# Joint mixer: attention by pairs of heads, turned modulation columns at the end, projection copies on ScalarE

## Chip, cores and metric

One core of a Trainium2 chip runs the whole program. The metric is device time of one execution in microseconds (us), the median of several runs. TensorE (PE) multiplies matrices, VectorE (DVE) and ScalarE (ACT) work on rows and on the banks that TensorE writes, GpSimd (POOL) works on rows in SBUF only, and SyncE (SP) issues the loads.

## What is computed

A float32 network of two blocks over 256 tokens of width 1024. The change touches the first layer of the second block, where 256 latent tokens and 256 context tokens are mixed by two mixers at once, from one projection:

```
aq, ak, av, ao, ag, bq, bk, bv = split_cols(h @ w_in)      # for latent and context tokens
h_ctx, h_lat = mlstm_bidirectional(...)                    # 4 heads of 128, both directions
k, q = rms_norm and rope of bk, bq                         # 8 query heads of 64, 2 key heads
b_lat = softmax([sink, q k_ctx, q k_band (windowed)]) @ v  # latent queries: 512 keys
b_ctx = softmax([sink, q_ctx k_ctx]) @ v_ctx               # context queries: 256 keys
mod   = silu(c) @ ada_w + ada_b                            # 12 parts of 1024 columns, two streams
```

The results of both mixers, side by side, go into the product with `w_out`. The modulation of this layer's later phases and of the next layer is computed in the same stage, since its 40 MB of weights have to be loaded some time.

## The kernel before

The program is one long sequence of phases. In each phase every engine has its own list of instructions, and the lists wait for each other by one counter per engine (`done(engine, phase, step, index)` is the count at which a step is finished). Dense products keep float32 accuracy with three products of split operands (lines 370 to 372); for each half slot of weights ScalarE makes the high part (`ahead`, line 357) and GpSimd the low part (line 364). Weights come through a ring of three slots of 1 MB, loaded by SyncE in the fixed order of `issue` (line 2902); a slot is loaded again when TensorE has read it.

**First projection ("2.0 in").** Six cuts of up to 512 columns, four pieces of 128 tokens each, numbered 0 to 23; a piece n is summed in bank n mod 7 and copied out by the `reader`: ScalarE for cut 4, else VectorE for even and ScalarE for odd pieces (lines 748 and 751). TensorE may start piece n when piece n - 7 is copied. Between the pieces stand the gates of the recurrent mixer (`mgate_rows_T`, `mgate_cols_T`), whose long chain of small steps runs on VectorE and ScalarE (`mgate_V`, lines 1981 to 2023), the norms of the query and key heads (`swa_prep`) and the turns of queries and keys to columns (`e0_turn`, `e1_turn`, line 860).

**The mix ("2.0 attention").** `both_of` weaves three generators on each engine, by turns: one piece of the recurrent mixer, one of the modulation, one of attention (none in each fifth turn). After 23 turns the recurrent mixer is done, and attention and modulation go on alone.

- Attention: 32 jobs, one for a head and a tile of 128 queries: first 16 over the context (256 keys, "narrow"), then 16 over latent tokens (512 keys and a mask, "wide"). At step s TensorE computes the scores of job s (line 918), turns the probabilities of job s - 3 (line 927) and multiplies those of job s - 4 with the values (line 942); VectorE takes the minimum of job s (scores are negated: lines 960, 964, 967) and scales the probabilities of job s - 2 (lines 975, 978, 981); ScalarE takes the exponentials of job s (lines 1006, 1009) and copies the turned probabilities of job s - 3 (line 1017). The probabilities have four buffers.
- Recurrent mixer: for each head h four products of queries and keys (`qk`, line 2069), which VectorE multiplies with decay tiles (line 2150) that ScalarE makes (lines 2100, 2103) from rows masked by GpSimd (line 2170), and two sums, one for each direction (line 2060), which VectorE finishes (`finish`, lines 2117 to 2134). One head takes five turns, a block.
- Modulation: 80 units, two for each 1 MB slot. `LATE_TURNS` says how many go into a turn. A part of eight units is summed in one of two banks, then VectorE adds the bias (line 1683), and TensorE turns four of six kinds of parts to columns (line 1691).

At the end TensorE turns the recurrent mixer's output (line 860), computes the gates' rows (line 1781) and starts the output projection.

## Time and profile before

| | |
|---|---|
| median of 3 runs | 1874.07 us (1873.81 to 1883.03) |
| the profiled execution | 1877.97 us, of which its span 1876.1 us |
| TensorE busy in the span | 1767.1 us |
| first product after the projection's wait | at 786.67 us |
| first modulation unit of the mix | at 866.74 us |
| first recurrent sums | at 895.03 us |
| first product of the output projection | at 1042.97 us |

Times in the rows are counted from the start of the span. A row of the timeline gives start, duration, engine, line, operation, output and inputs, how many instructions it merges, and in brackets how long the engine stood idle before and what released it. Durations of matmuls overlap: what one costs is the distance to the next start. A float32 matmul appears as two instructions.

### The profile page before, as it was taken

What the parts mean: (1) busy time and instruction counts of PE and PEld (TensorE: products, weight loads), DVE (VectorE), ACT (ScalarE), POOL (GpSimd) and SP (SyncE); (2) the same over time, 40 slices, a digit from 0 to 9 for tenths busy, and PEclk for the clock granted to TensorE, in tenths of its full rate; (3) what the DMA queues carried; (4) which work ended last, traced back from release to release, by engine and by line L of the source; (5) the groups of instructions that cost most, each with busy time, mean ns of one, the idle gap of its engine ahead of it and who ended that gap; (6) DMA issues with size and microseconds to landing.
All of it is one profiled execution on the core that took longest, in us unless ns stands there. A gap on an engine that the chain in (4) does not pass through costs nothing.

```text
span 1876.1 us, 25748 instructions
## 1 busy us (share of the span) xinstructions
PE 1767.1 (94%) x10058; PEld 1438.4 (77%) x10058; DVE 751.9 (40%) x1655; ACT 905.7 (48%) x1654; POOL 947.6 (51%) x416
## 2 busy tenths in 40 slices
PE   8999999998899999898998999999999898899998
PEld 6668998776688888785555888888888877678886
DVE  4543231244344453743567143343200443346631
ACT  4655454445566743433335354444422454457762
POOL 4645688774278885331015234444343341238886
PEclk9999999999899999999999999999999999999999
DMA  8336765443156653227875133333232430136654
GB/s 271 102 102 215 244 186 176 168 157 113 56 163 186 182 177 105 77 90 247 286 275 180 51 85 90 90 109 94 90 101 79 108 106 24 45 92 192 188 169 146
DMA packets 264843, 263.48 MB, mean 140 GB/s; under 512 B 11332, under 2 KB 202124, under 8 KB 264596
## 3 DMA queue, kind: packets, MB, share of 16 engines
q1 hardware_dynamic: 264435, 261.25, 45.0%
q8 instruction: 80, 1.31, 0.3%
q10 hardware_dynamic: 288, 0.59, 0.1%
q14 instruction: 40, 0.32, 0.1%
HBM read 260.76 MB, written 1.06 MB: 140 GB/s over the span
## 4 chain that ended last, share of the span: by engine, by line
PE 80%; DVE 7%; ACT 5%; DMA 5%; issue 2%; SPq 1%; POOL 0%; ACTq 0%; DVEq 0%
PE bank L370 18%; PE bank L371 18%; PE bank L372 17%; PE bank L1447 8%; PE bank L1448 4%; PE bank L1663 2%; PE bank L1251 2%; DMA weights<-in_ada_w 2%; ACT work L1369 1%; PE bank L1221 1%; ACT weights_high L357 1%; PE bank L2060 1%; PE bank L918 1%; PE bank L942 1%; DVE work L1330 1%
## 5 line engine op out<-in xcount | busy, mean ns | idle before, releaser
L364 POOL TENSOR_TENSOR weights_low<-weights,weights_high 128x1024 fp32r<-128x1024 f32 (+1 forms) x388 | 918.7, 2382 | 767.4 <-ACT weights_high L357 766.9
L357 ACT ACTIVATE weights_high<-weights 128x1024 fp32r<-128x1024 f32 (+1 forms) x388 | 401.6, 1046 | 377.8 <-PE bank L372 122.1
L370 PE MATMUL bank<-weights_high,normed_features_high_low 128*128 128x512 f32 (+4 forms) x752 | 288.9, 384 | 14.6 <-POOL weights_low L364 5.6
L372 PE MATMUL bank<-weights_low,normed_features_high_low 128*128 128x512 f32 (+4 forms) x752 | 273.8, 364 | 0.0
L371 PE MATMUL bank<-weights_high,normed_features_high_low 128*128 128x512 f32 (+4 forms) x752 | 273.7, 364 | 0.0
L1447 PE MATMUL bank<-normed_features_high_low,weights_high 128*128 128x512 f32 x704 | 249.4, 399 | 0.6 <-DVE normed_features_high_low L499 0.4
L370 PE MATMUL bank<-normed_features_high_low,weights_high 128*128 128x256 f32 (+1 forms) x704 | 237.9, 338 | 0.4 <-DVE normed_features_high_low L497 0.2
L371 PE MATMUL bank<-normed_features_high_low,weights_low 128*128 128x256 f32 (+1 forms) x704 | 236.5, 336 | 0.0
L372 PE MATMUL bank<-normed_features_high_low,weights_high 128*128 128x256 f32 (+1 forms) x704 | 236.5, 336 | 0.0
L1448 PE MATMUL bank<-normed_features_high_low,weights_low 128*128 128x256 f32 x704 | 197.7, 281 | 0.0
L370 PEld LDWEIGHTS bank<-weights_high,normed_features_high_low 128*128 128x128 f32 x752 | 144.9, 193 | 46.4 <-issue 13.6
L370 PE MATMUL bank<-weights_high,hidden_high 128*128 128x512 f32 x440 | 172.9, 393 | 2.8 <-DVE hidden_low_narrow L1525 1.0
L372 PE MATMUL bank<-weights_low,hidden_high 128*128 128x512 f32 x440 | 171.3, 389 | 0.0
L372 PEld LDWEIGHTS bank<-weights_low,normed_features_high_low 128*128 128x128 f32 x752 | 144.4, 192 | 21.3
L1447 PEld LDWEIGHTS bank<-normed_features_high_low,weights_high 128*128 128x128 f32 x704 | 132.3, 188 | 34.3 <-DVE normed_features_high_low L499 0.5
L371 PEld LDWEIGHTS bank<-weights_high,normed_features_high_low 128*128 128x128 f32 x752 | 145.1, 193 | 17.0
L370 PEld LDWEIGHTS bank<-normed_features_high_low,weights_high 128*128 128x128 f32 x704 | 133.6, 190 | 17.7 <-issue 3.3
L372 PEld LDWEIGHTS bank<-normed_features_high_low,weights_high 128*128 128x128 f32 x704 | 133.6, 190 | 13.6
L371 PEld LDWEIGHTS bank<-normed_features_high_low,weights_low 128*128 128x128 f32 x704 | 133.6, 190 | 13.5
L1448 PEld LDWEIGHTS bank<-normed_features_high_low,weights_low 128*128 128x128 f32 x704 | 133.0, 189 | 0.0
L371 PE MATMUL bank<-weights_high,hidden_low_narrow 128*128 128x512 f32 x264 | 102.8, 389 | 0.0
L370 PEld LDWEIGHTS bank<-weights_high,hidden_high 128*128 128x128 f32 x440 | 82.6, 188 | 23.3 <-POOL weights_low L364 2.2
(330 smaller groups left out, 2334.1 us busy)
## 6 DMA issues: line engine op xcount, KB each, us to landing
weights<-in_ffn_w_up SPq DMA_DIRECT2D x44, 1024.0 KB, 6.1
weights<-in_ffn_up SPq DMA_DIRECT2D x44, 1024.0 KB, 6.0
weights<-in_ada_w SPq DMA_DIRECT2D x40, 1024.0 KB, 6.3
weights<-in_ffn_w_down SPq DMA_DIRECT2D x20, 1024.0 KB, 5.1
weights<-in_ffn_down SPq DMA_DIRECT2D x20, 1024.0 KB, 5.0
weights<-in_diff_w_qkv SPq DMA_DIRECT2D x12, 1024.0 KB, 5.2
weights<-in_hyb_w_in SPq DMA_DIRECT2D x11, 1024.0 KB, 5.5
weights<-in_odd_w_in SPq DMA_DIRECT2D x9, 1024.0 KB, 5.2
```

The source lines that it names most:

```text
L357: A.eng.activation(high(whigh[:, m % HIGHS, :]), raw(wslot[:, u % SLOTS, :]), ACT.Copy).then_inc(scalar_done, A.one(("A", "high", m)))
L364: G.eng.tensor_tensor(raw(wlow[:, u % SLOTS, :]), raw(wslot[:, u % SLOTS, :]), high(whigh[:, m % HIGHS, :]).bitcast(F32), ALU.subtract).th ...
L370: T.eng.matmul(out_, lh, rh, start=first, stop=False)
L371: T.eng.matmul(out_, ll, rh, start=False, stop=False)
L372: return T.eng.matmul(out_, lh, rl, start=False, stop=last)
L918: i = T.eng.matmul(bank[:, a:b], l, r, start=(m == 0), stop=(m == len(terms) - 1))
L942: i = T.eng.matmul(o, l, r, start=(first and c == 0), stop=(last and c == nc_ - 1))
L1221: i = T.eng.transpose(psum[TURNED][:, at:at + P], way["probs"](buffer(way, q, x), n)[:, c * P:(c + 1) * P], ident)
L1251: i = T.eng.matmul(psum[SCORES[x]][:, a:b], l, r, start=(m == 0), stop=(m == len(terms) - 1))
L1447: T.eng.matmul(bank[:, 0:2 * n].rearrange("p (h t) -> p h t", h=2), wh, nTb[:, :, k, lo:lo + n], start=first, stop=False)
L1448: return T.eng.matmul(bank[:, 0:n], wl, nTh[:, k, lo:lo + n], start=False, stop=last)
L1663: i = T.eng.matmul(to[32 * j:32 * j + 32, :], silu_k[:, k, 2 - 2 * layer:34 - 2 * layer], w[:, a, j * MOD_N:(j + 1) * MOD_N], start=(k == ...
```

## The change

- `tile_pairs` makes 16 steps of two heads each out of the 32 jobs. A step has two halves, and each half is one turn of the weave. First half of step s: TensorE computes both heads' scores, alternately, into banks 3 and 4; VectorE takes both minima; ScalarE both exponentials, with the sink's. Second half: VectorE scales the pair s - 1, TensorE turns it in bank 0 (both heads at once when narrow; head 0, then head 1 after ScalarE's copy when wide), ScalarE copies it into a layout that joins the two tiles of queries, and when s - 2 is a second tile TensorE multiplies both heads of both tiles with the values.
- One denominator addition and one reciprocal serve a pair.
- The modulation is summed in one bank, and its six turned parts come together behind the last unit (after the recurrent mixer). `LATE_TURNS` starts with 2, 2, 2, 2 instead of 4, 2, 2, and has one more turn. VectorE takes its piece of modulation ahead of the recurrent one while the recurrent mixer runs.
- Cuts 2 and 3 of the first projection are copied by ScalarE alone; the turns of keys start one piece later; ScalarE splits weights up to half 14 inside the gates' chain; the table of exponentials is loaded before the last turns are copied. Head rows 2 and 3 are loaded one weight load later.
- The last mixer's routine (`pair_T`, `pair_V`, `pair_A`) gets its banks by argument and does the same as before.

```diff
-                    if n in (1, 2):
-                        issue.extend(("rows in", h) for h in (2 * n - 2, 2 * n - 1))
+                    if n in (1, 3):
+                        issue.extend(("rows in", h) for h in (n - 1, n))
...
+        SCORED, TURNED, SUMMED = (3, 4), 0, 7
...
+        def att_T(T, ph, steps):
+            count, held = len(steps), None
+            for s in range(count + 3):
+                if s < count:
+                    j = steps[s]
+                    if s >= 1:
+                        e = "V" if steps[s - 1]["mask"] is not None else "A"
+                        T.eng.wait_ge(SEM[e], done(e, ph, "read", s - 1, 1))
+                    for (a, b, terms), (_, _, others) in zip(j["heads"][0]["scores"], j["heads"][1]["scores"]):
+                        for m in range(len(terms)):
+                            for x, (l, r) in enumerate((terms[m], others[m])):
+                                i = T.eng.matmul(psum[SCORED[x]][:, a:b], l, r, start=(m == 0), stop=(m == len(terms) - 1))
...
                 yield
+                if 0 <= s - 1 < count:
+                    q = s - 1
+                    n = steps[q]["n"]
+                    for heads in heads_of(n):
+                        if held is not None:
+                            T.eng.wait_ge(scalar_done, done(*held))
+                        for x in heads:
+                            T.eng.wait_ge(vector_done, done("V", ph, "probs", q, x))
+                            for c in range(n // P):
+                                at = (x * n if len(heads) == 2 else 0) + c * P
+                                i = T.eng.transpose(psum[TURNED][:, at:at + P], rows_of(q, x, n)[:, c * P:(c + 1) * P], ident)
+                        i.then_inc(tensor_done, T.one(("T", ph, "turn", q, heads[-1])))
+                        held = ("A", ph, "turned", q, heads[-1])
+                if 0 <= s - 2 < count and steps[s - 2]["tile"] == 1:
...
+                    for c in range(n // P):
+                        for x, head in enumerate(j["heads"]):
+                            i = T.eng.matmul(psum[SUMMED][head["out"][0], 0:SEQ], head["v"][c], joined(g, n, x)[:, c, :], start=(c == 0), stop=(c == n // P - 1))
...
+        def att_V(V, ph, steps, aside):
...
+                for step in aside.get(s, []):
+                    step(V)
+                yield
+                if 0 <= s - 1 < count:
+                    q = s - 1
+                    b = 2 * (q % 2)
+                    den, r = mxs[:, 8 + b:10 + b], mxs[:, 24 + b:26 + b]
+                    V.eng.wait_ge(scalar_done, done("A", ph, "exp", q, 1))
+                    V.eng.tensor_tensor(den, den, mxs[:, 16 + b:18 + b], ALU.add).then_inc(vector_done, V.one())
...
+                    for x in range(2):
+                        pb = rows_of(q, x, steps[q]["n"])
+                        V.eng.tensor_scalar(pb, pb, r[:, x:x + 1], None, ALU.mult).then_inc(vector_done, V.one(("V", ph, "probs", q, x)))
...
-        LATE_BANKS = (0, 6, 0, 6, 0, 6, 0, 6, 1, 2)
-        LATE_TURNS = [4, 2, 2] + [3, 3, 2] * 7 + [2] * 8
+        LATE_TURNS = [2, 2, 2, 2] + [3, 3, 2] * 7 + [2] * 8
+        LATE_FLAT = [part for part in LATE_MOD if part[1] in FLAT]
+        late_sums, late_flat = psum[6][:, 0:MOD_N], (lambda i: psum[5][:, 16 * i:16 * i + 16])
...
+                    elif n % (2 * MOD_UNITS) == 0:
+                        T.eng.wait_ge(vector_done, done("V", "mod rows", *LATE_MOD[n // (2 * MOD_UNITS) - 1]))
...
+            T.eng.wait_ge(vector_done, done("V", "ml", "done"))
+            for i, part in enumerate(LATE_FLAT):
+                mod_flat_T(T, *part, late_flat(i))
+            yield
...
+                if d == 0:
+                    ahead(A, first_half["2.0 in"] + 14)
...
-        proj_phase("2.0 in", ("2.0 norm", ALL, shift_scale(0, 0)), EVEN_CUTS, lambda c: ALL, even_dst, lambda c, j: "A" if c == 4 else "VA"[j % 2],
+        proj_phase("2.0 in", ("2.0 norm", ALL, shift_scale(0, 0)), EVEN_CUTS, lambda c: ALL, even_dst, lambda c, j: "A" if c in (2, 3, 4) else "VA"[j % 2],
...
-                            4: [evac_step("2.0 turn", e0, range(8), LAST), exp_ready_A]})
+                            4: [exp_ready_A, evac_step("2.0 turn", e0, range(8), LAST)]})
...
-            both_of(att_A(A, ATTN, js + jl, {MOUT_AT[5]: [lambda A: heads_rms_A(A, "mo", TT * MH)], 31: [out_high(1)], 32: [out_high(2)], 33: [out_high(3)], 34: [out_high(4)]}),
+            both_of(att_A(A, ATTN, js + jl, {14: [lambda A: heads_rms_A(A, "mo", TT * MH)], 15: [out_high(1)], 16: [out_high(3)], 17: [out_high(4)]}),
```

## Rows read from the trace of the kernel before

**Rows 1.** The page, busy time, share of the span and instructions.
```profile
PE 1767.1 (94%) x10058; PEld 1438.4 (77%) x10058; DVE 751.9 (40%) x1655; ACT 905.7 (48%) x1654; POOL 947.6 (51%) x416
```

**Rows 2.** Timeline of the first projection: TensorE, VectorE, ScalarE.
```profile
786.67 0.80 PE L370 MATMUL bank<-weights_high,normed_features_high_low 128*128 128x512 f32 x1 [5.43 <-DVE big L748]
...
785.93 1.49 DVE L748 COPY big<-bank 128x512 f32<-128x512 f32 x2
...
778.41 1.29 ACT L751 ACTIVATE big<-bank 128x512 f32<-128x512 f32 x2
```

**Rows 3.** Stretches of the mix: busy time by engine, granted clock, DMA share, GB/s.
```profile
895.03:942.47 47.44, 43.82 (x385) 26.50 (x384) 29.39 (x93) 17.59 (x61) 5.01 (x4) 0.98 0.80 284
...
895.03:980.86 85.83, 78.90 (x670) 47.57 (x669) 49.76 (x168) 30.36 (x102) 5.01 (x4) 0.97 0.78 277
...
980.86:1035.18 54.32, 48.18 (x344) 29.11 (x343) 39.25 (x81) 26.95 (x61) 28.12 (x20) 0.92 0.53 175
...
866.74:895.03 28.29, 22.40 (x197) 10.57 (x197) 11.02 (x38) 11.55 (x41) 2.51 (x2) 0.92 0.95 358
```

**Rows 4.** TensorE's waits in the mix: us in total, times, longest.
```profile
PE bank L1663 <- DMA weights<-in_ada_w: 7.6, 7, 1.8
...
PE bank L1663 <- ACT big L751: 2.4, 1, 2.4
```

**Rows 5.** Timeline of TensorE in the mix.
```profile
921.39 1.50 PE L1663 MATMUL bank<-weights,silu_wide 128*32 128x256 f32 x24
...
922.82 0.70 PE L918 MATMUL bank<-qk_features 64*128 64x256 f32 x2
...
923.81 0.65 PE L942 MATMUL bank<-head_squares,big 128*64 128x128 f32 x4
...
924.39 2.50 PE L2060 MATMUL bank<-big,work 128*128 128x129 f32 x20
...
965.47 2.79 PE L1663 MATMUL bank<-weights,silu_wide 128*32 128x256 f32 x24
...
979.80 1.12 PE L918 MATMUL bank<-qk_features 64*128 64x512 f32 x2
```

**Rows 6.** Timeline of TensorE in the last mixer.
```profile
1542.68 1.95 PE L1276 MATMUL bank<-work,big 128*64 128x256 f32 x16
...
1546.18 0.63 PE L1221 MATMUL bank<-con,work 128*128 128x128 f32 x4
...
1546.74 1.13 PE L1251 MATMUL bank<-qk_features 64*128 64x512 f32 x4
...
1547.80 0.66 PE L1221 MATMUL bank<-con,work 128*128 128x128 f32 x4
```

**Rows 7.** Timeline of VectorE in the mix.
```profile
913.86 1.12 DVE L2119 SCALAR_TENSOR_TENSOR st<-st 128x4 f32<-128x4 f32 x1
...
919.35 0.42 DVE L964 TENSOR_REDUCE mxs<-bank 128x1 f32<-128x256 f32 x1
...
921.49 0.23 DVE L2117 COPY st<-bank 128x2 f32<-128x2 f32 x2 [0.88 <-PE bank L2060]
...
922.37 0.88 DVE L2130 TENSOR_TENSOR big<-bank,st 128x256 f32<-128x256 f32 x2
...
987.98 0.75 DVE L960 CUSTOM_DVE_ANT_0 attention_rows<-bank,con,nsink 128x512 f32<-128x512 f32 x1 [1.97 <-PE bank L918]
...
989.44 0.68 DVE L2196 TENSOR_REDUCE rms<-work 128x4 f32<-128x512 f32 x1
...
1020.22 2.23 DVE L975 TENSOR_TENSOR mxs<-mxs 128x1 f32<-128x1 f32 x1
```

**Rows 8.** Timeline of ScalarE in the mix.
```profile
930.50 0.47 ACT L1006 ACTIVATE attention_rows<-bank,mxs 128x256 f32<-128x256 f32 x1 [3.52 <-DVE mxs L967]
...
931.42 0.39 ACT L2100 ACTIVATE gate_rows<-work,mcol 128x128 f32<-128x128 f32 x1
...
932.40 0.79 ACT L2103 ACTIVATE gate_rows<-head_rows,mcol 128x128 f32<-128x128 f32 x2
```

More of the change, by code:

```diff
@@ new lines, in att_V @@
+        def att_V(V, ph, steps, aside):
+            count = len(steps)
+            for s in range(count + 3):
+                if s < count:
+                    j = steps[s]
+                    V.eng.wait_ge(tensor_done, done("T", ph, "turn", s - 2, 1))
+                    for x, head in enumerate(j["heads"]):
+                        b = 2 * (s % 2) + x
+                        mn = mxs[:, b:b + 1]
+                        bank = psum[SCORED[x]][:, 0:j["n"]]
+                        V.eng.wait_ge(tensor_done, done("T", ph, "scores", s, x))
+                        if j["mask"] is not None:
+                            V.eng.tensor_tensor_reduce(out=rows_of(s, x, j["n"]), in0=bank, in1=j["mask"], scale=1.0, scalar=head["sink"],
+                                                       op0=ALU.add, op1=ALU.min, accum_out=mn).then_inc(vector_done, V.one(("V", ph, "read", s, x)))
+                        else:
+                            V.eng.tensor_reduce(mn, bank, AX_X, ALU.min).then_inc(vector_done, V.one())
+                            V.eng.wait_ge(vector_done, V.n)
+                            V.eng.tensor_tensor(mn, mn, head["sink"], ALU.min).then_inc(vector_done, V.one())
+                        V.note(("V", ph, "max", s, x))
@@ L985, in att_V @@
-                if s >= LOW and jobs[s - LOW]["close"] is not None:
-                    j = jobs[s - LOW]
-                    src_cols, high, low = j["close"]
-                    if low is not None:
-                        V.eng.wait_ge(scalar_done, done("A", ph, "group", j["group"]))
-                        V.eng.tensor_tensor(low, psum[SUM_BANK][:, src_cols], high.bitcast(F32), ALU.subtract).then_inc(vector_done, V.one(("V", ph, "group", j["group"])))
-                yield
-        def att_A(A, ph, jobs, aside={}):
-            n = len(jobs)
-            for s in range(n + LOW):
+                yield
@@ L1011, in att_A @@
[L1011 to L1022 removed]
+                yield
@@ new lines, in att_A @@
+                if 0 <= s - 1 < count:
+                    q = s - 1
+                    j = steps[q]
+                    n, g = j["n"], j["group"]
+                    A.eng.wait_ge(tensor_done, done("T", ph, "sum", g - 2))
+                    tile = slice(j["tile"] * P, (j["tile"] + 1) * P)
+                    for heads in heads_of(n):
+                        A.eng.wait_ge(tensor_done, done("T", ph, "turn", q, heads[-1]))
+                        b = chunks(att_rows_b[:, 1024 * heads[0]:1024 * heads[0] + 1024]) if g % 2 == 0 else old_queries(heads[0])
+                        A.eng.activation(b[:, 0:len(heads) * n // P, tile], psum[TURNED][:, 0:len(heads) * n].rearrange("p (c q) -> p c q", q=P),
+                                         ACT.Copy).then_inc(scalar_done, A.one(("A", ph, "turned", q, heads[-1])))
@@ L1294, in pair_V @@
                         mn = mxs[:, b:b + 1]
-                        bank = psum[SCORES[x]][:, 0:j["n"]]
+                        bank = psum[way["scores"][x]][:, 0:j["n"]]
                         V.eng.wait_ge(tensor_done, done("T", ph, "scores", s, x))
@@ L2735, in both_of @@
             for u in range(1 + 5 * MH + 2):
+                if modulation_first:
+                    next(modulation, None)
                 next(recurrent)
-                next(modulation, None)
+                if not modulation_first:
+                    next(modulation, None)
                 if u % 5 != 4:
```

262 lines of the change are left out of this document (91 added, 171 removed).

## The prediction, made before the changed kernel was run

> **What bounds the kernel now.** I read the page first. TensorE is busy nearly all the span [rows 1], so an edit counts only if it takes work or waits off TensorE. I then cut the trace at the events that the change touches: the first projection of the joint block, and the mix up to the output projection's first product at 1042.97.
>
> In the projection, TensorE stands still once, for 5.43 us [rows 2]: it waits for a bank that VectorE is to copy out, and VectorE reaches that copy only at 785.93, at the end of the gates' scans. ScalarE had copied its pieces of the same cut at 778.41.
>
> In the mix, three stretches differ [rows 3]. Up to the first recurrent sums (895.03) TensorE is busy 22.4 of 28.3 us and the DMA engines have a 0.95 share: the modulation weights bound it, and the waits name them [rows 4]. From there to 980.86 it is busy 78.9 of 85.8 us: TensorE bounds it, and the rest is small waits. From 980.86 to 1035.18 it is busy 48.2 of 54.3; the idle part is in the last 15 us, where VectorE's probabilities come late.
>
> **The change, part by part.**
>
> *Projection copies.* Cuts 2 and 3 go to ScalarE, whose own pieces of cut 2 were out 7 us before VectorE's. Four copies where it did two cost it some 1.3 us more, under 21 us of matmuls per cut. The wait goes: -5.4. Bounds: 0 if ScalarE's halves or VectorE's head norms, which also come earlier only by 1.5 us, become the next wait; -6.5 with the slow first products after the wait [rows 2] gone too.
>
> *TensorE work of attention.* One score of 256 columns takes 0.63 us, of 512 columns 1.06 us (the rows of 0.70 and 1.12 less the 0.07 by which they overlap the next, [rows 5]). The pair routine that the last mixer already runs issues the two heads alternately, on different 64 rows, and both 512-column scores together take 1.06 us (1546.74 to 1547.80, [rows 6]). So eight wide pairs save 8 x 1.06 = 8.5 us, eight narrow ones 8 x 0.63 = 5.0. Sums over 128 columns take 0.58 us per narrow job (923.81 to 924.39) and 1.02 per wide one; joined over both tiles, sixteen instructions take 1.88 [rows 6]. Four wide groups save 4 x (4.08 - 1.88) = 8.8, four narrow ones 4 x (2.32 - 0.94) = 5.5. Transposes of narrow pairs save some 1. Together 29 us of TensorE work.
>
> *The new ring.* This is what I hold against those 29 us. Before, TensorE turned a job's probabilities three steps after its scores, and VectorE had finished them a step earlier. Now both are done in the second half of one step: VectorE must take the two minima of the pair just scored, do the recurrent piece of its next turn, and only then scale the pair before, for which TensorE waits. Nothing is a step ahead in that ring.
>
> I walk one block of five turns from [rows 5, 7, 8]. In the turn with the recurrent sums, TensorE needs 2.43 for them (the row of 2.50, less the overlap) and 1.4 for modulation (24 instructions, 921.39 to 922.82), 3.8 us in all, before the transposes; VectorE waits for the sums (2.5), takes 1.8 us to finish them (921.49 to 923.25) and 1.0 to scale: 5.3. TensorE waits 1.4. Two turns later TensorE is ready after 2.5 us. On the other side stand, from the scores on: 0.75 for the first minimum (0.42, a comparison with the sink, two hand-overs), 1.3 for ScalarE's two exponentials with their sink terms (0.66 each), its decay tiles (1.8, from 931.42 to 933.2), then VectorE's second half of the recurrent product (0.7) and its scaling (1.0): 5.5. TensorE waits 3. A block before has 43.8 / 2 = 21.9 us of TensorE work [rows 3]; less 2.9 for two narrow pairs and 0.6 for column turns it is 18.4. With 1.4, 3 and 0.6 in smaller waits behind them it is 23.4. Twice, GpSimd's masks fall on VectorE's short operations, which take 1.1 us instead of 0.16 (913.86, [rows 7]). Before, half of that ended in slack; in the ring all 2 us count: 25.4. Three blocks, the third wide but without masks: 25.4 + 25.4 + 24.9 = 75.7 (1.5 us for two wide scores and a wide transpose). The last two turns, with two more sums and the first wide pairs, take 12.6. That is 88.3 for what took 85.8: +2.5. Bounds: -17 (29 us spread evenly over the pairs give 16 here) and +7.
>
> *VectorE against GpSimd.* The rows of 913.86 and 1020.22 [rows 7] show operations of 0.16 us held up for 1.1 and 2.2 us while GpSimd works. The Trainium skill (SBUF, "two separate sides") calls the port pair of the two an exclusive lock that whoever starts first holds for the whole instruction. By that alone VectorE would win about as often as it loses, and the middle would be 2 us shorter, 1868; by the rows it loses, 1870.
>
> *Start and units.* The modulation's first unit waits no more for ScalarE's copy (2.4, [rows 4]), and 16 instead of 19 units are taken before the first sums. In a stretch bound by DMA that is 1.5 MB less at some 3.2 us per MB (358 GB/s over the stretch [rows 3] are 2.9, and SyncE issues a load only when a slot of three is read). 2.4 + 4.8 = 7.2; I take -7. Three fewer units here are three more later, counted above and below. Bounds: -2.4 (the ring binds here) and -9.
>
> *Wide pairs at the end.* The turned bank is one. The second head's transposes wait until ScalarE has copied the first's: 1.62 us from start to start in the last mixer [rows 6], with scores in between there, with nothing here: 1.0 idle per pair. In front of the first head's transposes TensorE has 1.0 us of modulation; VectorE needs 2 x 0.67 for the minima [rows 7] and 0.9 for the scaling, and at four steps 0.68 more for a mean square that now stands in between (989.44), with some 0.7 lost to GpSimd. Along the ring a pair takes 2.45 (to the probabilities) + 1.62 + 0.6 + 0.9 (half a group's sum) + 1.0 + 1.1 = 7.7, and 9.1 at the four, against 2 x 3.66 = 7.3 before (one job: 1.06 + 0.58 + 1.02 + 1.0). Five pairs: 44 us (with two table loads for the root at step 14). After the last scores 14.5 us: six turned column groups (2.6), two pairs' transposes and two sums, with the weights' splits of the output projection in front of ScalarE's copies. Before, 15.7 us passed from the last scores to 1035.18, mostly VectorE held up by GpSimd for 2.2 us at a time (1020.22, [rows 7]). 58.6 against 54.3: +4.3. Bounds: -9 (only TensorE's work counts) and +10.
>
> *The turned columns at the end.* They take 2.5 us of small matmuls out of the weave and put them behind the last scores, and the modulation now has one bank: each part waits for VectorE's addition of the part before (0.42), mostly while TensorE would wait in the ring anyway. Both are in the walks.
>
> *Moved at no cost.* SyncE now issues the four loads of head rows 2 and 3 one weight load later (before the fourth unit, not the third): they are read a block of 23 us later, and the queue in front of the next weights is the same length. ScalarE makes two weight halves inside the gates' chain, where it waits for VectorE anyway, and loads the table for exponentials before the last column turns instead of after them; the cover there is TensorE's products, and without it each is 1.3 us. The merging of two reciprocals into one per pair takes 0.3 us a pair off VectorE, in the walks.
>
> *Clock.* Longer waits let the granted clock fall. After 2.2 us idle, 24 modulation matmuls took 2.79 us instead of 1.50 (965.47, [rows 5]), so one fall costs some 1.3 us. The granted clock is already 0.92 to 0.97 over the three stretches [rows 3]. I add +2 for a few more. Bounds 0 and +15.
>
> Sum: -5.4 - 7 + 2.5 + 4.3 + 2 = -3.6 us. From the profiled span of 1876.1 (1877.97 in all; the median of the runs is 3.9 lower, 1874.07) this gives a span near 1872.5, and for the median 1870.
>
> **The rivals.**
>
> *The ring has more slack than I count* (TensorE's work decides). For it: VectorE is busy only 50 of 86 us in the middle [rows 3], so it could run far less late than in my walk. Then the middle falls by some 10 us, the end by 5, the start and the projection keep theirs: -28; with the DMA engines (0.78 share already) holding back part of it, -20. Time 1854. Against it: the order of the waits, which no busy share changes.
>
> *The clock turns it round* (the other side). Each block has one wait of 3 us, each wide pair one of 1.5 to 2.2 and one of 1. If a fall follows most of them, 12 falls at 1.3 us are +16 instead of +2: 1884. It decides from nine additional falls on. Against it: the first stretch has seven waits for DMA, up to 1.8 us long [rows 4], and keeps 0.92. The Trainium skill (TensorE: Matmul & The Clock Gate, on oscillation) describes just this: a loop that waits for data in every round is throttled again in every round. By it every block would pay; the fall at 965.47 fits.
>
> *The projection keeps its wait* (that part doesn't do what it is for): ScalarE is bound by its waits for VectorE's gate chain and copies late, 0 instead of -5.4: 1875.
>
> **How the numbers follow.** A measurement of this kernel tells a difference from none at about 0.5%, 9.4 us. My forecast has 0.45 (own range 1862 to 1879), the slack 0.29 (1846 to 1864), the clock 0.18 (1878 to 1892), the kept wait 0.08. Faster by over 0.5%: all of the slack case and a little of mine, 0.33. Slower by over 0.5%: most of the clock case and a little of mine, 0.20. Same: 0.47. To leave out no more than 2 in 10 the range is 1851 to 1884.
>
> **What would show it.** The 5.43 us wait of the projection is gone. The first recurrent sums start 7 us earlier relative to the start of the mix. Blocks of sums stand 23 to 25 us apart, with TensorE's transposes waiting for VectorE's scaling, 1 to 3 us each, 16 times; the second head's waits for ScalarE, 1 us, 8 times. TensorE busy in the mix falls by some 25 us and its idle time grows as much. Blocks under 21 us would mean the slack case; a granted clock under 0.85 over the mix, the clock case. It would be wrong above all if VectorE's part of the ring is half as long as walked.

## The result, and the profile after

The changed kernel takes 1891.84 us (median of 7 runs, 1884.9 to 1895.21), the kernel before took 1874.07 beside it. The ratio is 1.009, with a 95% interval of 1.0066 to 1.0114: slower by nearly 1%. The forecast was 1870 with a range of 1851 to 1884. The profiled execution of the changed kernel has a span of 1889.6 us (1891.43 in all). One execution of a later kernel (the best one with filler) took 2346.57 us at a granted clock of 0.697, and the numbers given for that kernel leave it out.

The page has TensorE 13.7 us less busy than before [rows 1], and yet the span is longer:

```profile
PE 1753.4 (93%) x9962; PEld 1422.2 (75%) x9962; DVE 740.1 (39%) x1619; ACT 906.9 (48%) x1650; POOL 948.4 (50%) x416
```

To see where the time went, cut both traces at the same events: the projection's first product, the first scores of the mix, the first recurrent sums, the scores of the last pair beside the recurrent part (before: the job's at 979.80), the turns of the recurrent output, the output projection's first product.

| stretch | before | after | difference |
|---|---|---|---|
| projection to first scores | 714.62 to 863.69: 149.1 | 712.13 to 853.43: 141.3 | -7.8 |
| to first recurrent sums | to 895.03: 31.3 | to 880.36: 26.9 | -4.4 |
| "middle", to the last scores beside the recurrent part | to 979.80: 84.8 | to 972.48: 92.1 | +7.4 |
| "last stretch", to the turns of the recurrent output | to 1035.18: 55.4 | to 1051.18: 78.7 | +23.3 |
| to the output projection | to 1042.97: 7.8 | to 1059.12: 7.9 | +0.1 |

These five come to +18.6 us, the spans differ by 13.5. The changed kernel's trace is 5.1 us shorter ahead of 712.13 and behind 1059.12 together, where both kernels do the same work. So a single trace has a spread of its own. The middle shows how much: seven of the kernels below and above have the same instructions there (the changed kernel and those with filler, two modulation banks, old copies, small GpSimd work, banks without scaling first, scaling first only late), and it takes 92.1 to 95.9 us, at granted clocks of 0.93 to 0.88. A difference under some 4 us between two traces' stretches tells nothing by itself.

The windows of the changed kernel, middle and last stretch (columns as in [rows 3]):

```profile
880.36:972.48 92.12, 70.71 (x643) 41.83 (x641) 46.74 (x151) 30.97 (x98) 5.17 (x5) 0.93 0.74 268
972.48:1051.18 78.70, 55.15 (x317) 27.76 (x313) 32.84 (x76) 27.22 (x61) 27.45 (x20) 0.64 0.44 147
```

In the last stretch TensorE is busy 55.15 us although it has fewer instructions than before (317, where [rows 3] has 344 in 48.18 us), and the granted clock is 0.64, where [rows 3] has 0.92. Length less busy time is 23.6 us of standing still. The view of the waits says for what (over the mix: us in total, times, longest):

```profile
PE bank L931 <- DVE attention_rows L979: 24.2, 12, 4.3
PE bank L1659 <- DVE mod L1679: 10.8, 4, 3.9
PE bank L1659 <- DMA weights<-in_ada_w: 7.7, 4, 4.1
PE bank L931 <- ACT big L1019: 4.5, 4, 2.3
PE bank L931 <- ACT attention_turned L1019: 3.3, 4, 1.0
```

L931 are the transposes, L979 VectorE's scaling of the probabilities, L1659 the modulation's products, L1679 VectorE's addition that frees the single modulation bank, L1019 ScalarE's copy of turned rows. Three waits follow each other on one ring: for the modulation bank, for the scaling, for ScalarE's copy. TensorE's timeline shows two pairs of it:

```profile
982.34 2.08 PE L917 MATMUL bank<-qk_features 64*128 64x512 f32 x4
987.26 1.93 PE L1659 MATMUL bank<-weights,silu_wide 128*32 128x256 f32 x16 [2.84 <-DVE mod L1679]
989.48 1.09 PE L931 MATMUL bank<-con,attention_rows 128*128 128x128 f32 x4 [0.29 <-DVE attention_rows L979]
991.32 1.12 PE L931 MATMUL bank<-con,attention_rows 128*128 128x128 f32 x4 [0.75 <-ACT big L1019]
992.36 3.34 PE L942 MATMUL bank<-attention_turned,big 128*64 128x256 f32 x16
995.63 1.07 PE L1659 MATMUL bank<-weights,silu_wide 128*32 128x256 f32 x16
996.63 1.13 PE L917 MATMUL bank<-qk_features 64*128 64x512 f32 x4
997.69 1.07 PE L1659 MATMUL bank<-weights,silu_wide 128*32 128x256 f32 x16
1001.48 0.63 PE L931 MATMUL bank<-con,attention_rows 128*128 128x128 f32 x4 [2.71 <-DVE attention_rows L979]
1002.88 1.09 PE L931 MATMUL bank<-con,attention_rows 128*128 128x128 f32 x4 [0.78 <-ACT big L1019]
1003.90 1.94 PE L1659 MATMUL bank<-weights,silu_wide 128*32 128x256 f32 x16
1005.76 2.08 PE L917 MATMUL bank<-qk_features 64*128 64x512 f32 x4
```

From scores to scores it is 14.3 us, then 9.1. The same instructions appear in two lengths: four score instructions take 1.13 or 2.08, sixteen of modulation 1.07 or 1.93, a head's transposes 0.63 or 1.12. They are at half speed behind the waits, but not always at once: the transposes at 1001.48 still take 0.63 us behind a wait of 2.71, and only the next group takes twice its time. VectorE in the first of these pairs:

```profile
984.56 0.75 DVE L958 CUSTOM_DVE_ANT_0 attention_rows<-bank,con,nsink 128x512 f32<-128x512 f32 x1 [6.12 <-PE bank L917]
985.24 0.75 DVE L958 CUSTOM_DVE_ANT_0 attention_rows<-bank,con,nsink 128x512 f32<-128x512 f32 x1
985.91 0.68 DVE L2186 TENSOR_REDUCE rms<-work 128x4 f32<-128x512 f32 x1
986.69 0.42 DVE L1679 TENSOR_TENSOR mod<-bank,mod 128x256 f32<-128x256 f32 x1
987.03 0.69 DVE L973 TENSOR_TENSOR mxs<-mxs 128x2 f32<-128x2 f32 x1
987.76 0.17 DVE L975 RECIPROCAL mxs<-mxs 128x2 f32<-128x2 f32 x1
987.96 2.79 DVE L979 TENSOR_SCALAR attention_rows<-attention_rows,mxs 128x512 f32<-128x512 f32 x2
```

VectorE stands still 6.12 us for the scores of the new pair, with ScalarE done with the exponentials of the old pair since 976.4, and only after the new pair's two minima, a mean square and the modulation's addition does it scale the old pair, for which TensorE waits, so that the next scores come late again. That is the ring, seen from inside.

### The profile page after: what moved, and what is told of

Its sections match the earlier page's. It is cut to its first block, busy times and chain, and to the rows that moved or that the text cites. A ratio compares the mean times of both kernels' runs of the same rounds, so it can differ in the third digit from the quotient of the medians.

```text
span 1889.6 us, 25466 instructions
## 1 busy us (share of the span) xinstructions
PE 1753.4 (93%) x9962; PEld 1422.2 (75%) x9962; DVE 740.1 (39%) x1619; ACT 906.9 (48%) x1650; POOL 948.4 (50%) x416
## 4 chain that ended last, share of the span: by engine, by line
PE 72%; DVE 12%; ACT 8%; DMA 5%; issue 2%; POOL 1%; SPq 1%; DVEq 0%; ACTq 0%
PE bank L370 17%; PE bank L371 17%; PE bank L372 17%; PE bank L1443 5%; PE bank L1444 3%; ACT weights_high L357 2%; PE bank L1247 2%; PE bank L1659 2%; ACT work L1365 1%; PE bank L1217 1%; DMA weights<-in_ffn_w_up 1%; PE bank L931 1%; DMA weights<-in_ada_w 1%; PE bank L942 1%; PE bank L2050 1%
## 5 line engine op out<-in xcount | busy, mean ns | idle before, releaser
L371 PEld LDWEIGHTS bank<-normed_features_high_low,weights_low 128*128 128x128 f32 x704 | 133.6, 190 | 13.5
L370 PEld LDWEIGHTS bank<-weights_high,hidden_high 128*128 128x128 f32 x440 | 82.6, 188 | 23.3 <-POOL weights_low L364 2.0
```

The source lines that it names most:

```text
L370: T.eng.matmul(out_, lh, rh, start=first, stop=False)
L371: T.eng.matmul(out_, ll, rh, start=False, stop=False)
```

## The experiments

Twelve kernels, each timed in five rounds beside the kernel before on the same chip. Middle and last stretch are cut at the same events as above; "clock" is the granted clock of the last stretch; "scaling" is TensorE's wait for VectorE's scaling over the mix. All but the kernel with copies alone are the changed kernel with an edit, and "best" is the one with VectorE scaling first, the modulation banks and the second turned bank. The median of the kernel before lay between 1872 and 1874 each time, so differences are taken from the ratios.

| run | median us | ratio to before (95%) | middle | last | clock | scaling |
|---|---|---|---|---|---|---|
| before | 1872 to 1874 | 1 | 84.8 | 55.4 | 0.92 | 6.1 |
| changed kernel | 1891.84 | 1.0090 (1.0066 to 1.0114) | 92.1 | 78.7 | 0.64 | 24.2 |
| filler | 1884.88 | 1.0065 (1.0047 to 1.0083) | 94.3 | 71.3 | 0.86 | 20.3 |
| scaling first | 1877.83 | 1.0016 (1.0 to 1.0032) | 82.0 | 75.3 | 0.70 | 1.6 |
| two modulation banks | 1892.37 | 1.0105 (1.0087 to 1.0122) | 94.6 | 76.9 | 0.72 | 31.6 |
| old copies | 1898.27 | 1.0136 (1.0116 to 1.0155) | 92.7 | 78.7 | 0.64 | 24.4 |
| scaling first + modulation banks | 1865.09 | 0.9956 (0.9937 to 0.9975) | 81.3 | 61.3 | 0.82 | 1.6 |
| ... + second turned bank | 1852.84 | 0.9886 (0.9864 to 0.9909) | 80.7 | 49.0 | 0.87 | 3.2 |
| ... + filler | 1862.91 | 0.9940 (0.9916 to 0.9963) | 81.1 | 59.4 | 0.91 | 1.6 |
| small GpSimd work | 1884.86 | 1.0057 (1.0036 to 1.0078) | 94.3 | 69.6 | 0.74 | 19.3 |
| banks without scaling first | 1883.69 | 1.0066 (1.0049 to 1.0083) | 93.3 | 68.1 | 0.77 | 35.0 |
| best, later splits | 1851.24 | 0.9894 (0.9877 to 0.9912) | 81.9 | 46.6 | 0.85 | 2.8 |
| before, with the copies alone | 1866.3 | 0.9968 (0.9955 to 0.9981) | | | | 3.8 |
| best, scaling first only late | 1863.47 | 0.9954 (0.9938 to 0.9971) | 95.9 | 47.3 | 0.89 | 19.0 |

**Filler in the last stretch** (`e1_filler`): is it the clock?

```diff
                     for heads in heads_of(n):
...
+                        if s >= 11:
+                            warm_T(T, 1, 8 if heads[0] == 0 else 4)
```

> The changed kernel, with filler: from attention step 11 on, TensorE multiplies the identity by itself (128x128, results read by nobody) 8 times ahead of a pair's first transposes and 4 times ahead of the second head's, in a bank that the recurrent part has left. No wait and no order changes. If the low granted clock of the last stretch (0.64 over 973.5 to 1051.2 of the changed kernel) is what costs there, it rises above 0.85, products of 24 and 16 instructions take their full-speed durations again, and the stretch falls from 77.6 to some 65 us: the time falls by 9 to 13 us. If the waits themselves cost (VectorE's scaling late in the ring), the filler only lies inside them, and the time falls by less than 3 us or rises.

The clock of the stretch rose to 0.86 as both theories allow, but the stretch fell only from 78.7 to 71.3 and the ratio by 0.0025, with intervals that overlap. The waits for the scaling went from 24.2 to 20.3 us over the mix, in the stretch from 10.1 to 5.6, where filler now stands in their place. The filler isn't free (its instructions, busy us, mean ns):

```profile
L437 PE MATMUL bank<-con 128*128 128x128 f32 x144 | 23.3, 325 | 0.0
```

TensorE is busy 58.47 us in the stretch, 23.3 of them with filler, so its own work takes some 35 us and not 55.15. Most of the half speed is gone, and the time hardly follows, because the filler fills the waits and in part more: where TensorE had waited for the modulation bank, sixteen filler instructions took 3.58 us at half speed ahead of transposes whose scaling VectorE ended at 1018.19, a microsecond before the filler did. The stretch is still 15.9 us above the 55.4 of before, but how much of that is filler this run doesn't say. So the 7.4 us is, within the spread of a trace, a lower bound for the clock's part of the 23.3, and what a full clock without filler would give stays open here.

**VectorE scales first** (`e2_scale_first`): is it the ring? The twelve lines that scale pair s - 1 move from behind the `yield` of step s to the head of the step.

```diff
             for s in range(count + 3):
+                if 0 <= s - 1 < count:
+                    q = s - 1
...
+                        V.eng.tensor_scalar(pb, pb, r[:, x:x + 1], None, ALU.mult).then_inc(vector_done, V.one(("V", ph, "probs", q, x)))
                 if s < count:
                     j = steps[s]
```

> The changed kernel, with one move on VectorE: it scales the probabilities of pair s-1 at the start of step s, before the minima of pair s, and no longer after them in the second half of the step. If the ring without slack is the cause, TensorE's waits for the scaling (24.2 us in 12 waits) shrink to under 8 us, the blocks of recurrent sums come to 21 to 23 us apart instead of 24.6 to 29.7, and the time falls by 20 to 30 us, below the kernel before. If the clock alone costs, the waits shrink but the stretch stays at half speed and less than 8 us come back. If the wait is only passed on (VectorE's minima now come later, so ScalarE's exponentials and the next scores do), the total of TensorE's waits stays within 5 us of what it was and the time too.

The waits for the scaling fell from 24.2 to 1.6 us, and the middle from 92.1 to 82.0, 2.8 below the kernel before. The granted clock of the middle is as it was (0.92 for 0.93) and TensorE's busy time too (69.87 us for 70.71), so there the waits alone account for the 10 us. Overall the ratio fell by 0.0074, 13.9 us, to no difference from before; the 20 to 30 us expected did not come. But the last stretch hardly moved (78.7 to 75.3): there other waits took the place.

```profile
PE bank L1659 <- DVE mod L1679: 10.8, 6, 3.2
PE bank L1659 <- DMA weights<-in_ada_w: 10.3, 6, 5.6
PE bank L2059 <- DVE work L2140: 6.0, 4, 2.3
PE bank L931 <- ACT big L1019: 5.8, 4, 2.3
PE bank L931 <- ACT attention_turned L1019: 5.1, 3, 3.6
PE bank L931 <- DVE mxs L954: 4.0, 1, 4.0
```

The ring theory is right in the middle, and incomplete at the end. The wait of 4.0 named after VectorE is also one for the turned bank, as far as order tells: it stands in front of the second head's transposes at 969.30, and VectorE had scaled that pair by 965.9. ScalarE copied the first head's turned rows only at 968.67, behind the exponentials of the next pair, for which it had waited until VectorE's minima at 966.6. That is the price of the new order: VectorE's minima come later.

**Two banks for the last modulation parts** (`e3_two_banks`): is it the single bank?

```diff
-        late_sums, late_flat = psum[6][:, 0:MOD_N], (lambda i: psum[5][:, 16 * i:16 * i + 16])
+        late_sums, late_flat = (lambda g: psum[(6, 1, 2)[max(0, g - 7)]][:, 0:MOD_N]), (lambda i: psum[5][:, 16 * i:16 * i + 16])
...
+                    elif n == 8 * 2 * MOD_UNITS:
+                        T.eng.wait_ge(vector_done, done("V", "ml", "done"))
+                    elif n % (2 * MOD_UNITS) == 0 and n < 8 * 2 * MOD_UNITS:
```

> The changed kernel, with the last two modulation parts summed in banks 1 and 2, which the recurrent part has left, so that neither waits for VectorE's addition of the part before. If the single bank costs by itself, the two waits of 2.84 us in the last stretch go and bring the clock with them: the time falls by 5 to 8 us. If VectorE's lateness is the cause, TensorE reaches the transposes earlier and waits there for the scaling instead: the waits for the scaling grow by what these two lose, and the time stays within 2 us.

The waits for the modulation bank fell by 5.8 us (10.8 to 5.0) and those for the scaling grew by 7.4 (24.2 to 31.6), all of it in the last stretch (10.1 to 17.6); the ratio did not fall. The wait was passed on, as the second theory has it: alone, this bank costs nothing.

```profile
PE bank L931 <- DVE attention_rows L979: 31.6, 12, 4.3
PE bank L1659 <- DVE mod L1679: 5.0, 2, 3.8
```

**Old copies** (`e4_old_copies`): what is the projection's part worth?

```diff
-... lambda c, j: "A" if c in (2, 3, 4) else "VA"[j % 2],
+... lambda c, j: "A" if c == 4 else "VA"[j % 2],
```

> The changed kernel, with the projection's part undone: cuts 2 and 3 are copied by VectorE and ScalarE in turn, and the column turns and the table load stand where they stood. If that part is worth what its wait was, the time rises by 5 to 6 us and the wait of 5.4 us in the projection is back. If the start of the mix, bound by the modulation weights, swallows it, the time stays within 2 us. If it had been worth more than the wait (what follows the wait at half clock), it rises by 8 to 10.

The column turns, the table load and ScalarE's early weight half go back to their old places too. The wait is back and the ratio rises by 0.0046, 8.6 us, at the upper expectation; the last stretch is the same to a hundredth (78.70 us).

```profile
PE bank L370 <- DVE big L748: 5.4, 1, 5.4
```

**Scaling first and modulation banks** (`e5_first_banks`), the two edits above together.

> VectorE scales the pair before first, as in the run with that one move, and the last two modulation parts are summed in banks 1 and 2 as well. With VectorE early, TensorE has nothing to wait for where those two waits of 2.84 us go: if VectorE's lateness was what swallowed the two banks when they were tried alone, now some 4 to 8 us come back against the move alone (1877.8), 1870 to 1874. If ScalarE's copies of the turned rows are what comes last in a pair, the waits move there and the time stays within 2 us of the move alone.

The ratio fell by a further 0.0060, 11 us, more than expected, and the last stretch from 75.3 to 61.3. Of these 14.0 us, 10.4 are TensorE's busy time (53.17 to 42.76, clock 0.70 to 0.82) and 3.7 less standing still. The same bank edit that was worth nothing alone is worth this once VectorE scales in time.

**A second bank for turned rows** (`e6_two_turned`), on top. The columns of the turned modulation parts, which had bank 5, move to the unused half of bank 6.

```diff
+        turned_bank = lambda q, heads: 5 if q >= 10 and heads == (1,) else TURNED
...
-                            T.eng.wait_ge(scalar_done, done(*held))
+                            T.eng.wait_ge(scalar_done, done(*held[to]))
```

> As the run before it, and in the last stretch (from pair 10 on) the second head's transposes go to bank 5, so that they don't wait until ScalarE has copied the first head's. If the single turned bank is the step that holds a wide pair, TensorE's waits for ScalarE's copies (10.9 us with the move alone) fall under 4 us, the clock of the last stretch rises from 0.70, and the time comes to 1858 to 1866, below the kernel before. If ScalarE itself is late (its copies stand behind the exponentials of the next pair), the waits move to the sums and the time falls by less than 3 us.

1852.84 us, ratio 0.9886, which beats both kernels. The windows, middle and last stretch:

```profile
882.79:963.53 80.74, 70.19 (x643) 41.09 (x641) 44.95 (x147) 30.67 (x98) 5.02 (x4) 0.94 0.83 294
963.53:1012.51 48.98, 37.86 (x317) 20.07 (x313) 35.51 (x76) 25.96 (x61) 26.79 (x20) 0.87 0.68 237
```

The last stretch has 317 matmul instructions, as in the changed kernel, and they take 37.86 us of busy time, not 55.15. This difference of 17.3 us is what the lower clock (0.64 against 0.87) added to the instructions' own time there, but for the small part that overlaps. One pair now follows the other without a wait for an engine:

```profile
980.65 1.13 PE L919 MATMUL bank<-qk_features 64*128 64x512 f32 x4
981.71 1.07 PE L1664 MATMUL bank<-weights,silu_wide 128*32 128x256 f32 x16
982.71 1.09 PE L936 MATMUL bank<-con,attention_rows 128*128 128x128 f32 x8
983.73 1.07 PE L1664 MATMUL bank<-weights,silu_wide 128*32 128x256 f32 x16
984.73 1.13 PE L919 MATMUL bank<-qk_features 64*128 64x512 f32 x4
```

Both heads' transposes stand together (x8, 1.09 us) and the pair takes 4.1 us, 7.6 with the sums.

**The same with filler** (`e7_all_filler`).

> As the run before it, and with filler: 8 products of the identity ahead of a pair's first transposes and 4 ahead of the second head's, from step 11 on, in the bank that the transposes then overwrite. If the clock still stands below 0.85 in the last stretch and costs, the time falls by a further 3 to 8 us. If the waits are gone, the filler has nothing to lie in and costs its own length: 12 products take 1.5 us a pair at full clock, so the time rises by up to 9 us.

The clock rose to 0.91 and the ratio by 0.0054, 10 us. The filler takes 20.2 us in the stretch, 2.8 us a pair (972.76 to 974.65 and 975.08 to 975.98) and not the 1.5 expected, and the stretch is 10.5 us longer: where few waits are left, filler costs more than it gives back. The low clock of this stretch follows from the waits: it went from 0.64 to 0.87 as they were taken away, without any filler.

**GpSimd's work cut** (`e8_small_pool`): how much of VectorE's lateness is GpSimd's doing? The squares, gains, gates and scale of the recurrent outputs are computed for 8 of 512 columns; the kernel leaves out the rest, so its results are wrong.

```diff
-                G.eng.tensor_tensor(h, h, head_g[:, :], ALU.mult)
+                G.eng.tensor_tensor(h, h, head_g[:, 0:8], ALU.mult)
```

> The changed kernel, with GpSimd's work on the recurrent outputs (squares, gains, gates and scale) cut from 512 to 8 columns each; the rest of those columns is left uncomputed. If GpSimd holding up VectorE is a large part of the last stretch's loss, VectorE's scalings take 0.88 us for two throughout (2.50 and 2.79 in the changed kernel), the waits for them shrink by 5 us or more, and the time falls by 6 to 12 us. If it is only what I counted (0.7 us a pair where the two meet), it falls by 1 to 4. If the output projection waits for GpSimd's last scale at the end, up to 3 us come on top.

The scalings fell from a mean of 933 to 484 ns, the waits for them by 4.9 us, the last stretch by 9.1, the ratio by 0.0033, 6 us (intervals overlap). TensorE's two waits for the modulation bank keep their 5.7 us in the stretch (the trace names them after L973 here), so GpSimd doesn't cause those. In the profile of the changed kernel and then of this one, VectorE in the last stretch (count, busy us, mean ns):

```profile
L979 DVE TENSOR_SCALAR attention_rows<-attention_rows,mxs 128x512 f32<-128x512 f32 x14 | 12.5, 933 | 0.2
L973 DVE TENSOR_TENSOR mxs<-mxs 128x2 f32<-128x2 f32 x7 | 2.9, 420 | 0.0
```
```profile
L979 DVE TENSOR_SCALAR attention_rows<-attention_rows,mxs 128x512 f32<-128x512 f32 x14 | 6.2, 484 | 0.2
L973 DVE TENSOR_TENSOR mxs<-mxs 128x2 f32<-128x2 f32 x7 | 1.0, 144 | 0.0
```

**Banks without scaling first** (`e9_banks_only`): the two bank edits on the changed kernel, with VectorE's order as it is.

> The best kernel so far (1852.8) without VectorE's early scaling: the last two modulation parts in banks 1 and 2 and the second head's transposes in bank 5 from pair 10 on, but VectorE scales after the next pair's minima, as in the changed kernel. If VectorE's order is what closes the ring, the banks bring little: waits for the scaling stay at 25 to 35 us and the time stays at 1884 to 1890. If the banks were the cause and VectorE's order only added to it, the last stretch falls by 20 us and the time to 1868 to 1874.

The ratio is 1.0066, and the waits for the scaling are the largest of all runs. So the banks alone bring 4.5 us (intervals overlap), and together with VectorE's order 38: the order is the link that has to go first.

```profile
PE bank L936 <- DVE attention_rows L984: 35.0, 18, 4.3
```

**Later splits** (`e10_late_splits`): the best kernel, ScalarE's splits of the output projection's weights behind its last copies.

```diff
-15: [out_high(1)], 16: [out_high(3)], 17: [out_high(4)]}
+17: [out_high(3)], 18: [out_high(4)]}
```

> The best kernel so far, with ScalarE's splits of the output projection's first weights moved behind its last copies of turned rows (steps 17 and 18 instead of 15 to 17). In its trace TensorE waits 1.21 and 1.67 us there and runs at half clock behind them. If the splits in front of the copies cause this, the time falls by 2 to 5 us, to 1848 to 1851. If the output projection then waits for GpSimd's low halves of the weights (2.35 us each for four), the time rises by up to 5 us.

The last stretch went from 49.0 to 46.6, within the spread of single traces, but the wait of the gates' rows for VectorE's low halves grew from 1.9 to 3.2 and their products went to half speed (5.41 us instead of 3.72). The two ratios cannot be told apart.

**The copies alone** (`e11_before_copies`): the kernel before with the projection's part of the change and nothing else.

> The kernel before, with the projection's part of the change alone: cuts 2 and 3 copied by ScalarE, the column turns one step later, the table load ahead. If its worth is the same in both kernels, as undoing it in the changed kernel showed (6 to 8 us), the time is 1865 to 1867. If the mix of the kernel before, whose modulation waited 2.4 us for ScalarE's last copy, gives part of it back, 1868 to 1871.

Ratio 0.9968, 6 us faster. In place of the 5.4 us TensorE now waits 3.1 us for the gates' columns, where the changed kernel waits 1.3. From the projection's first product to the first scores it takes 141.5 us, as the changed kernel does (141.3); to the first recurrent sums it takes 33.4 where the kernel before took 31.3, so the mix gives some back.

**Scaling first only late** (`e12_first_late`): the best kernel, but with VectorE's new order only from step 11 on.

> The best kernel so far, with VectorE's early scaling only from step 11 on; in the steps beside the recurrent part it scales after the minima, as in the changed kernel. If the middle's loss is VectorE's order there, the stretch from the first recurrent sums to the last scores beside the recurrent part is again 91 to 93 us instead of 81 to 82 and the time is 1861 to 1864. If the recurrent part's own waits for VectorE bound the middle, both orders take about the same there and the time stays within 3 us of 1852.8.

The middle is 95.9 us again, the last stretch 47.3, the ratio 0.9954: 12.7 us above the best. VectorE's order beside the recurrent part is worth 15 us of the middle between these two traces, some 13 of the time. The other runs bear it out: the middle takes 80.7 to 82.0 us in the five kernels that scale first there and 92.1 to 95.9 in the seven that don't.

## Why the prediction was wrong, point by point

**Projection: -5.4 forecast, -7.8 in the traces, 6 to 8.6 in the two runs that isolate or undo it.** The mechanism was right. The term left out the speed afterwards: the granted clock from 750 to 800 us is 0.97 and from 800 to 850 us 0.99 in the changed kernel, and 0.93 in both stretches before. A new wait of 1.3 us for the gates' columns was not foreseen.

**Start and units: -7 forecast, -4.4 in the traces.** Fewer units before the first sums are there, but the DMA share of that stretch is 0.89 and TensorE waits up to 4.1 us for one modulation load. It lies inside the bounds, and the traces of six kernels with the same instructions there have 26.9 to 29.5 us, so the size is no sharper than that.

**Middle: +2.5 forecast, +7.4 (the other traces with the same middle have up to +11).** The walk was right in kind: sums stand 25.7, 29.7 and 24.6 us apart against the 25.4 of the walk, and TensorE waits for the scaling there, mostly 1.2 to 3.6 us. What it lacked is the single modulation bank: TensorE waits 3.94 us at 931.92 and 1.19 at 950.78 for VectorE's addition, and behind the first of these 24 instructions take 2.79 us. The text had this "mostly while TensorE would wait in the ring anyway". In the last stretch that was true (the run with two banks); in the middle nothing tested it by itself, since no bank is free there.

**Last stretch: +4.3 forecast with bounds of -9 and +10, +23.3 measured.** This is the step that failed, together with the next: the two terms gave +6.3 where the stretch grew by 23.3. The sequence of waits was mostly as walked, and the second head's wait for ScalarE was 0.75 to 1.03 us, once 2.28, where I took 1.0. The walk gave 7.7 us for the first pair and 9.1 for each of the four with a mean square in between, 44 in all, with the sums spread evenly; the pairs stand 9.9, 14.3, 9.1, 14.5 and 9.3 apart, 57.1 in all. The long ones are those with the sums and with a wait of 2.84 for the modulation bank, which the walk had at no cost. From the end of the last scores it had 14.5 us, and 19.6 passed (1031.56 to 1051.18). Half speed covers this excess:

```profile
1031.56 5.29 PE L1687 MATMUL bank<-con,mod 128*128 128x8 f32 x24
1039.58 3.62 PE L942 MATMUL bank<-attention_turned,big 128*64 128x256 f32 x16
1047.57 3.68 PE L942 MATMUL bank<-big 128*64 128x256 f32 x16 [0.69 <-ACT big L1019]
```

The walk had 2.6 for the first of these and 1.88 for each of the others. So three things were off. GpSimd holding up VectorE was put at 0.7 us in four pairs; the scalings of four pairs alone took 6.3 us longer than 0.88 each, and taking most of GpSimd's work away shortens the stretch by 9.1 us (clock 0.64 to 0.74 included). The single modulation bank was put at nothing; that holds as long as VectorE scales late, and once it scales early the bank is worth 11 us. And the walk used full-speed durations throughout. The code shows where room was lost: from its step 21 on the kernel before took turns between three banks for scores and two for turned rows, where the changed kernel has one for each head's scores and one for turned rows. What the score banks were worth was not tried.

**Clock: +2 forecast with bounds of 0 and +15.** The price of a fall was taken from one place, 24 modulation products behind one wait: 1.3 us. In the ring there is a wait in front of most groups, and a fall slows scores, transposes and sums too. Between the changed kernel and the best one the same 317 instructions differ by 17.3 us in busy time. How much of this would come back with the waits left in place is less: filler brought back 7.4 us of the stretch, net of what it cost itself. The two figures are not one quantity, since longer instructions partly fill waits that would be there anyway. How the 23.3 us split between waits and clock is not shown: the waits bring the clock down, and no run has these waits at full clock without filler.

**The rivals.** "The clock turns it round" had 0.18 and 1884, and is the closest: under 0.85 over the mix was named as its sign, and the clock over the mix is 0.80. But it was put as an addition to a ring near balance, and the runs show both at once. "The ring has more slack" is refuted by the waits. "The projection keeps its wait" did not happen. The Trainium skill (TensorE: Matmul & The Clock Gate, on oscillation) describes a loop throttled again in every round by waits; the trace agrees, with half-speed and full-speed durations by turns within each pair. The forecast's own sign, that TensorE's busy time in the mix falls by some 25 us, did not come: it fell by 5.3 us, since the lower clock put back what the change had taken out, and the idle time grew by 31.7.

**SBUF.** I had set the lock rule of the Trainium skill (SBUF, "two separate sides") against the rows as a case in which VectorE wins about as often as it loses. In the last stretch its scalings are held up in four of seven pairs (1.77 to 2.79 us for the two, 0.88 in the others), for a reason in the code: VectorE's own mean square (985.91) releases GpSimd's next three products, which then stand exactly where VectorE scales; so it is in three of the four. GpSimd in that pair:

```profile
986.67 1.04 POOL L2173 TENSOR_TENSOR work<-big 128x512 f32<-128x512 f32 x1 [9.23 <-DVE rms L2186]
987.78 1.27 POOL L2175 TENSOR_TENSOR big<-big,head_g 128x512 f32<-128x512 f32 x1
989.13 1.33 POOL L2177 TENSOR_TENSOR big<-big 128x512 f32<-128x512 f32 x1
```

VectorE's addition of 987.03 ends at 987.72, when GpSimd's first product ends (987.71); its two scalings run to 990.75, past the end of the third (990.46). The trace agrees with the Trainium skill here: whoever starts first holds. What decides here who does is the order of the releases.

**What the change could have had.** TensorE's saving of some 29 us was roughly real. In the changed kernel the clock hides it (150.94 us busy over the mix at a mean clock of 0.80, against 156.23 at 0.94 before); in the best one, with the same instructions at 0.91, TensorE is busy 131.47 us, 24.8 less than before (854.22 to 1020.05). With three links opened (VectorE's order, the modulation bank, the turned bank) the whole change is worth 21.3 us by the ratio, of which the copies are 6 to 8.6. Why the middle stays at 81 us, only 4 below before, was not tried: the largest waits left in the best run are 12.5 us over the mix for the modulation's weights from DMA and 5.7 for VectorE's products with the decay tiles.

## What to carry to other kernels

When work is restructured so that one engine both reads the new item and finishes the old one in the same step, let it finish the old one first: what others wait for goes ahead of what starts the next round. A ring with several links can give nothing back when a later one is opened first, so an edit that measures as nothing (a bank, a buffer) should be tried again after the first link is open. Price TensorE's work in a ring with a wait in each round at full and at half speed, and don't let an engine release, just ahead of its own critical operation, another that shares its ports.

## What the runs showed of the hardware

The granted clock of the last stretch lay between 0.64 and 0.89 in runs whose TensorE work there was the same, and TensorE's instructions took up to 1.9 times as long (1.95 and 3.68 us for the sixteen instructions of the same sums). Over a middle of the same instructions it lay between 0.88 and 0.93 from one execution to the next, and the stretch between 95.9 and 92.1 us. Filler products raised it from 0.64 to 0.86 while the kernel's time fell by 0.0025 of the ratio only, and from 0.87 to 0.91 while the time rose by 10 us: a higher mean clock is no gain by itself.
